# Column units as matmul pairs of 512 and 256 columns, their row scales later, and the first loads in quarters and halves

## The reference

```
x = x + 0.5 * swiglu(rms_norm(x), w_gate, w_up, w_down)        # "ffn1", inner width 2816
p = rms_norm(x) @ w_in                                          # "mix": RWKV-7 recurrence and pooled windows
x = x + concat(time_mix(p), pool_mix(p)) @ w_out
x = rms_norm(x + 0.5 * swiglu(rms_norm(x), ...))                # "ffn2", final norm of block 1
proj = rms_norm_2(x) @ w_in_2                                   # "mix2": rotary, sliding-window and differential attention
x = x + attention(proj) @ w_out_2
x = x + cross_attention(rms_norm_2(x), rms_norm_2(mem), w_cq, w_ckv, w_co)     # "mem", "cross"
x = x + square(relu(rms_norm_2(x) @ w_up)) @ w_down             # "mlp", inner width 4096
return rms_norm_2(x)
```

## Time and profile before

| | |
|---|---|
| median of three runs | 1076.35 us (1074.59 to 1076.88) |
| the profiled execution | 1075.12 us, of which the span from first to last instruction is 1073.2 us |
| PE busy | 1012.0 us, 94% of the span |
| DVE / ACT / POOL busy | 62% / 46% / 7% of the span |
| HBM read | 152.28 MB, 143 GB/s over the span |

### The profile page before, as it was taken

The page is one execution under the profiler, slowest core; times in us unless marked ns, Lnnn a source line. Parts: engine busy times, 40 slices in busy tenths (PEclk is TensorE's granted clock), DMA queues, the critical chain, the costliest instruction groups (busy, mean ns, idle before and its releaser), DMA issues.

```text
span 1073.2 us, 18930 instructions
## 1 busy us (share of the span) xinstructions
PE 1012.0 (94%) x7020; PEld 930.7 (87%) x7020; DVE 663.3 (62%) x1005; ACT 490.2 (46%) x806; POOL 70.5 (7%) x79
## 2 busy tenths in 40 slices
PE   7999999899799899999999999999999998999997
PEld 6899999798688886899999988998888887999996
DVE  4665555578894753765555577677646446555554
ACT  5544444566122121644444374533745545445542
POOL 3002000002240320000000000000300000000000
PEclk9999999999899999999999999999799998999999
DMA  6777656453310100576666746454034236565661
GB/s 200 213 238 219 185 178 190 122 158 100 97 41 2 39 2 1 167 209 192 178 191 179 235 118 190 140 169 161 20 98 138 79 99 196 180 191 178 194 190 64
DMA packets 204896, 154.01 MB, mean 144 GB/s; under 512 B 5947, under 2 KB 190624, under 8 KB 204848
## 3 DMA queue, kind: packets, MB, share of 16 engines
q1 hardware_dynamic: 203760, 151.35, 47.5%
q0 software_dynamic: 1088, 2.00, 0.7%
HBM read 152.28 MB, written 1.05 MB: 143 GB/s over the span
## 4 chain that ended last, share of the span: by engine, by line
PE 52%; ACT 3%; DVE 2%; DMA 1%; issue 1%; DVEq 0%; ACTq 0%
PE ps L458 52%; DMA raw<-in_w_ckv 1%; ACT XT L1062 1%; ACT arena L1047 1%; DVE wlo L1392 0%; ACT whi L1026 0%; PE ps L529 0%; ACT L1039 0%; DVE X L1411 0%; PE ps L792 0%; DVE X L1461 0%; DVE arena L1848 0%; DVE arena L1844 0%; ACT SMALL L1049 0%; DVE arena L1786 0%
## 5 line engine op out<-in xcount | busy, mean ns | idle before, releaser
L458 PE MATMUL ps<-XT,whi 128*128 128x256 f32 x2880 | 533.5, 287 | 7.7 <-DVE XT L1437 7.7
L458 PEld LDWEIGHTS ps<-XT,whi 128*128 128x128 f32 x2880 | 458.6, 193 | 17.6 <-issue 6.6
L1392 DVE TENSOR_TENSOR wlo<-raw,whi 128x1024 fp32r<-128x1024 f32 x280 | 343.7, 1231 | 151.5 <-ACT whi L1026 148.9
L458 PE MATMUL ps<-XT,wlo 128*128 128x256 f32 x1440 | 409.2, 284 | 0.0
L1026 ACT ACTIVATE whi<-raw 128x1024 fp32r<-128x1024 f32 x280 | 293.2, 1055 | 215.3 <-PE ps L458 127.7
L458 PEld LDWEIGHTS ps<-XT,wlo 128*128 128x128 f32 x1440 | 277.8, 193 | 0.0
L458 PE MATMUL ps<-whi,H 128*128 128x512 f32 x608 | 179.0, 395 | 5.9 <-DVE H L1952 4.0
L458 PE MATMUL ps<-arena 128*128 128x128 f32 (+7 forms) x1160 | 145.8, 298 | 14.0 <-DVE arena L1661 5.5
L458 PEld LDWEIGHTS ps<-arena 128*128 128x128 f32 (+3 forms) x1160 | 133.4, 192 | 28.1 <-DVE arena L1661 5.8
L458 PEld LDWEIGHTS ps<-whi,H 128*128 128x128 f32 x608 | 110.5, 191 | 25.5 <-DVE H L1952 4.2
L458 PE MATMUL ps<-wlo,H 128*128 128x512 f32 x304 | 96.0, 394 | 0.0
(11 more groups left out here) (232 smaller groups left out, 641.8 us busy)
## 6 DMA issues: line engine op xcount, KB each, us to landing
raw<-in_ffn_w_gate SPq DMA_DIRECT2D x44, 512.0 KB, 4.1
raw<-in_ffn_w_up SPq DMA_DIRECT2D x44, 512.0 KB, 3.8
raw<-in_ffn_w_down SPq DMA_DIRECT2D x44, 512.0 KB, 4.0
raw<-in_w_in SPq DMA_DIRECT2D x36, 512.0 KB, 3.9
raw<-in_w_up SPq DMA_DIRECT2D x32, 512.0 KB, 4.6
raw<-in_w_down SPq DMA_DIRECT2D x32, 512.0 KB, 3.5
raw<-in_w_out SPq DMA_DIRECT2D x16, 512.0 KB, 3.4
raw<-in_w_ckv SPq DMA_DIRECT2D x16, 512.0 KB, 5.1
```

The source lines that it names most:

```text
L458: return pe.matmul(o, st, mv, start=start, stop=stop, skip_group_check=True)
L1392: dve.tensor_tensor(wlo[:, n % RING, :], raw[:, n % RAW, :], whi[:, n % RING, :].bitcast(F32), sub).then_inc(lo_ready, 1)
```

## The change

- `a_unit`: per piece c one matmul of `whi` by all 512 columns of `XT[:, c, :]` into the whole bank, and one of `wlo` by the upper 256. The two halves of the bank are added afterwards: ACT copies the upper half of the bank out (`GL`, `UL`, `WLOW`, `CLOW`), DVE adds the lower half of the bank to it, and the row factor is multiplied in by a further instruction (ffn, mix, w_ckv keys), or folded into a later one (rotary tables, the copies of the values, the exponent's scale in cross).
- `row_scale` comes later: behind both units of chunk 0 in ffn, behind unit 2 in mix, behind unit 1 on mem; in cross it goes.
- mix: the multiplication by the row factor moves to POOL (`scale_rows`, 14 of 128 x 256), and the shift's two DVE instructions for unit k come one iteration later.
- x is loaded in four pieces and the first two units in two each, in the order x, gate, x, gate, up, up, and these are split as halves as they land; `wake` puts 8 and 10 small matmuls of constants ahead of the first real ones.
- `norm_hi` and `norm_lo` of mix, ffn2 and cross come ahead of the one split that stood before them; in mlp the sums go between chunks 1, 2 and 3, and `norm_scale` behind the last chunk.

```diff
@@ -382,10 +389,24 @@
...
-                sp.dma_start(X[:, tt, :], t["x"][0, tt * P:(tt + 1) * P, :]).then_inc(x_in[tt], 16)
-            for n in range(RAW):
-                load(n, 0, cols(("ffn1_w_gate", "ffn1_w_up")[n % 2], (n // 2) * P))
+            def load_half(n, h, src, landed):
+                dst = raw[:, n, 512 * h:512 * h + 512].rearrange("p (c n) -> p c n", c=KC // 2)
+                sp.dma_start(dst, src[:, 4 * h:4 * h + 4, :]).then_inc(landed, 16)
+            def load_x(h):
+                for tt in range(NT):
+                    sp.dma_start(X[:, tt, 512 * h:512 * h + 512],
+                                 t["x"][0, tt * P:(tt + 1) * P, 512 * h:512 * h + 512]).then_inc(x_in[2 * h + tt], 16)
+            load_x(0)
+            load_half(0, 0, cols("ffn1_w_gate", 0), raw_first[0])
+            load_x(1)
+            load_half(0, 1, cols("ffn1_w_gate", 0), raw_full[0])
+            load_half(1, 0, cols("ffn1_w_up", 0), raw_first[1])
+            load_half(1, 1, cols("ffn1_w_up", 0), raw_full[1])
+            load(2, 0, cols("ffn1_w_gate", P))
             def load_ffn(b, pre, first):
...
@@ -460,14 +481,19 @@
             def a_unit(n, dn, bank, after=None):
-                pe.wait_ge(lo_ready, n + 1 + dn)
+                halves = after == "ffn1" or (n == 1 and dn == 0)
+                if not halves:
+                    pe.wait_ge(lo_ready, n + 1 + dn)
                 s = n % RING
                 for c in range(KC):
+                    if halves and c == 0:
+                        pe.wait_ge(lo_first, n + 1)
+                    if halves and c == KC // 2:
+                        pe.wait_ge(lo_ready, n + 1)
                     if after and c % 2 == 0:
                         pe.wait_ge(xt_ready, 4 * NTP[after] + c // 2 + 1)
                     cs = slice(c * P, (c + 1) * P)
-                    mm(bank[:, 0:T], whi[:, s, cs], XT[:, c, 0:T], start=(c == 0), stop=False)
-                    mm(bank[:, 0:T], whi[:, s, cs], XT[:, c, T:2 * T], start=False, stop=False)
+                    mm(bank[:, :], whi[:, s, cs], XT[:, c, :], start=(c == 0), stop=False)
                     last = mm(bank[:, 0:T], wlo[:, s, cs], XT[:, c, 0:T], start=False, stop=(c == KC - 1))
                 last.then_inc(unit_used, 1)
...
@@ -538,8 +564,6 @@
                     if J + j >= 2:
                         pe.wait_ge(h_ready, J + j - 1 + dj)
                     a_unit(b + n, dn, PS[4 + j % 2], after)
-                    if after:
-                        row_scale(PS[0], RRB_N[after])
                     a_unit(b + n + 1, dn, PS[6 + j % 2])
                 def down(j, n, dn=0, dj=0, **k):
@@ -547,6 +571,7 @@
                     b_unit(b + n, dn, H[:, j % 2, :], **k)
                 gate_up(0, 0, after=("ffn1", "ffn2")[f])
+                row_scale(PS[0], RRB_N[("ffn1", "ffn2")[f]])
                 gate_up(1, 2)
                 pe.wait_ge(rrb_ready, RRB_N[("ffn1", "ffn2")[f]])
                 down(0, 4, start=True)
@@ -596,7 +621,7 @@
                     if i >= 4:
                         pe.wait_ge(w_sum, i - 3)
                     a_unit(B_WIN + i, 0, PS[W_BANKS[i % 4]], None if i else "mix")
-                    if i == 0:
+                    if i == 2:
                         row_scale(PS[0], RRB_N["mix"])
                     if i == 4:
                         pe.wait_ge(rrb_ready, RRB_N["mix"])
...
@@ -799,7 +824,7 @@
                     if i >= 4:
                         pe.wait_ge(c_sum, i - 3)
                     a_unit(B_CKV + i, 0, PS[Q_BANKS[i % 4]], None if i else "mem")
-                    if i == 0:
+                    if i == 1:
                         row_scale(PS[6], RRB_N["mem"])
                     if i == 5:
                         pe.wait_ge(rrb_ready, RRB_N["mem"])
...
+            def wake(n):
+                for k in range(n):
+                    mm(PS[k % 2][0:64, 0:P], ONES[:, 0:64], ONES)
+            pe.wait_ge(warm_set, 2)
+            wake(8)
             pe.wait_ge(const_in, 16)
             pe.wait_ge(first_in, 16)
             pe.transpose(PS[7][:, 0:KC], FIRST, ident[0:KC, 0:KC]).then_inc(vec_tp, 1)
+            wake(10)
             pe.wait_ge(vec_ready, 1)
             norm_t("ffn1")
             ffn(B_FFN1, 0)
...
@@ -1079,7 +1120,15 @@
                                 splits.n = n + 1
                     next_split(0)
+                    act.wait_ge(unit_used, b + n_gate + 1 + dn)
+                    if J + j >= 2:
+                        act.wait_ge(g_raw, J + j - 1 + dj)
+                    act.activation(GL[:, q, :], PS[4 + q][:, T:2 * T], ACT.Copy).then_inc(g_low, 1)
                     next_split(1)
+                    act.wait_ge(unit_used, b + n_up + 1 + dn)
+                    if J + j >= 2:
+                        act.wait_ge(u_sum, J + j - 1 + dj)
+                    act.activation(UL[:, q, :], PS[6 + q][:, T:2 * T], ACT.Copy).then_inc(u_low, 1)
                     act.wait_ge(g_sum, J + j + 1 + dj)
                     if J + j >= 2:
                         act.wait_ge(h_val, J + j - 1 + dj)
...
+            def low(i, n, bank, dst, sem_low, sem_sum, base=0):
+                split_to(n + LEAD + 1)
+                act.wait_ge(unit_used, n + 1)
+                if base + i >= 2:
+                    act.wait_ge(sem_sum, base + i - 1)
+                act.activation(dst[:, i % 2, :], bank[:, T:2 * T], ACT.Copy).then_inc(sem_low, 1)
             def deviation(wv):
...
@@ -1127,7 +1184,7 @@
             def mix():
                 row_scale(RRB_MIX, PS[0], RRB_N["mix"])
                 for i in range(N_WIN):
-                    split_to(B_WIN + i + LEAD + 1)
+                    low(i, B_WIN + i, PS[W_BANKS[i % 4]], WLOW, w_low, w_sum)
...
                 split_to(B_MLP + LEAD)
-                for j in range(3):
-                    chunk(j)
+                chunk(0)
+                chunk(1)
+                norm_sums(7, X, 6, [0])
+                chunk(2)
+                norm_sums(7, X, 6, [1])
                 with act.Fori(0, 9) as i:
...
@@ -1356,24 +1423,26 @@
             act.wait_ge(warm_set, 1)
             act.activation(SMALL[:, 346:347], WARM, ACT.Sqrt)
             act.wait_ge(const_in, 16)
-            split_to(1)
             act.wait_ge(vec_ready, 1)
             norm_hi("ffn1", "ffn1_norm")
+            split_half(1, 0)
+            split_half(1, 1)
+            splits.n = 2
+            split_to(3)
             norm_sums(0, X, 0)
             ffn(B_FFN1, 0)
             act.wait_ge(vec_ready, 2)
+            norm_hi("mix", "mix_norm")
             split_to(B_WIN + LEAD)
-            norm_hi("mix", "mix_norm")
             norm_sums(1, X, 1)
             mix()
...
-            norm_hi("ffn2", "ffn2_norm")
             norm_sums(2, X, 2)
...
             attention()
             cross()
             norm_hi("mlp", "g_mlp_2")
-            norm_sums(7, X, 6)
             mlp()
             norm_sums(8, X, 7)
...
@@ -1478,14 +1555,18 @@
                                 splits.n = n + 1
                     next_split(0)
-                    dve.wait_ge(unit_used, b + n_gate + 1 + dn)
+                    dve.wait_ge(g_low, J + j + 1 + dj)
                     if J + j >= 2:
                         dve.wait_ge(silu, J + j - 1 + dj)
-                    dve.tensor_tensor(GS[:, q, :], PS[4 + q][:, 0:T], RRB_FFN, mul).then_inc(g_sum, 1)
+                    dve.tensor_tensor(GS[:, q, :], PS[4 + q][:, 0:T], GL[:, q, :], add).then_inc(g_raw, 1)
+                    dve.wait_ge(g_raw, J + j + 1 + dj)
+                    dve.tensor_tensor(GS[:, q, :], GS[:, q, :], RRB_FFN, mul).then_inc(g_sum, 1)
                     next_split(1)
-                    dve.wait_ge(unit_used, b + n_up + 1 + dn)
+                    dve.wait_ge(u_low, J + j + 1 + dj)
+                    dve.tensor_tensor(US[:, q, :], PS[6 + q][:, 0:T], UL[:, q, :], add).then_inc(u_sum, 1)
+                    dve.wait_ge(u_sum, J + j + 1 + dj)
                     dve.wait_ge(silu, J + j + 1 + dj)
-                    dve.tensor_tensor(HS[:, q, :], PS[6 + q][:, 0:T], SG[:, q, :], mul).then_inc(h_val, 1)
+                    dve.tensor_tensor(HS[:, q, :], SG[:, q, :], US[:, q, :], mul).then_inc(h_val, 1)
                     dve.wait_ge(h_val, J + j + 1 + dj)
                     dve.wait_ge(h_hi, J + j + 1 + dj)
                     dve.tensor_tensor(H[:, q, T:2 * T], HS[:, q, :], H[:, q, 0:T].bitcast(F32),
...
+                def shift(k):
+                    dst = LBUF[:, k, :] if k < 2 else PV[:, k - 10, :] if k >= 10 else (PK, PR)[k % 2][:, (k - 2) // 2, :]
+                    mu = vec("mu_tail") if k == 1 else vec("mu_shift", WIN_COLS[k] // P)
+                    now, before = WRAW[:, k % 2, 1:T + 1], WRAW[:, k % 2, 0:T]
+                    dve.wait_ge(w_scaled, k + 1)
+                    dve.tensor_tensor(WDF[:, k % 2, :], before, now, sub).then_inc(own_dve, own.next())
+                    dve.wait_ge(own_dve, own.n)
```

(57 more changed lines are left out.)

139 lines of the change are left out of this document (86 added, 53 removed).

## The result

The changed kernel takes 1086.41 us (median of four runs, 1084.54 to 1087.26) against 1075.56 for the kernel before beside it (1074.59 to 1076.88). The ratio is 1.0098, with a 95% interval of 1.0078 to 1.0118. Forecast were 1073.2 us and a range of 1060 to 1083, so it is slower where faster was the likeliest, and outside the range. The profiled execution has a span of 1082.8 us against 1073.2. That of before is one of its faster ones: its granted clock is 0.979, where 24 of the 29 executions of before that were run beside the second group of experiments have 0.973 to 0.977.

A forecast was written before the change was run, and what follows sets the result against it. PE's pace was taken to bound mid-ffn1, with waits for DVE and ACT at joints and in mix. Terms -2.5 -3.6 +16 -1.2 -3.8 +1.5 +2.5 -2.6 -9.4 gave -3.1: 1073.2 us, range 1060 to 1083.

The forecast's parts named there:

- The pairs: Column units: a piece takes 0.349 us instead of 0.360, saving 0.09 per unit; ffn1 -3.6, ffn2 -3.8.
- Rival C: Column units: the pair doesn't pay and 113 path units lose their 0.09 us; 1083.4, chance 0.08.
- mem and w_in_2: Stages mem and w_in_2: no gain, PE's wait behind rope_args grows to about 6 us; +2.5, bounds 0 and +5.
- mlp: Stage mlp: wait before chunk 0 and half clock behind it go, 31 units get cheaper; -9.4 us, bounds -6 and -10.5.
- (a): Mix: row factors ready after unit 2 instead of unit 0, at 216.4 us instead of 214.26.
- (b): Mix: `w_mix` 2 takes three DVE iterations instead of two, 225.5 us instead of 220.2; PE waits 6.5.
- (d): Mix: `w_mix` 10 is raised one iteration later, ACT's activations follow the scans; K2 at 268.4 us instead of 257.16.
- (e): Mix: more POOL pauses and four multiplications, less what DVE waits for POOL today; +2.5 us.
- (c): Mix: POOL's products stretch DVE's iterations from 2.46 to 3.13 us, so the scans begin later; +3.7.
- Rival D: Start: the wake matmuls delay it by 2 us instead of the gain; 1077.7, chance 0.06.
- Rival A: Mix: the added work fits in DVE's and ACT's gaps, -5 us instead of +16; 1052, chance 0.13.
- Rival B: Mix and behind rope_args: granted clock falls longer than priced, 11.6 us instead of 3.0; 1082, chance 0.17.

The follow-up runs named there:

- second profile of after: The changed kernel run once more, unchanged, beside the kernel before: ratio 1.0075.
- the run with the kept parts: Changed kernel with column units of mix, mem and w_in_2 as before, mix's split ahead of the norm, mlp's sums between chunks 30 and 31: 0.9870 of before.

## Why the prediction was wrong

The sum was -3.1 and the trace has +9.6, 12.7 more; the second profile of after has +6.8. The table of joints says where, and the runs say why. No single term carries the miss: the pair is the largest one that is the same in every profile.

- **The pairs: the step that failed first, a term mis-sized (4.9 us).** "Per piece 0.229 + 0.120" took each interval from a stream of its own kind. Next to each other they are 0.236 + 0.117. 0.057 per unit instead of 0.09 is 1.3 less in ffn1 and 1.6 in ffn2. In mlp a unit and its row unit save 0.027 together, since there the row unit's matmuls, which were not changed, take 0.232 instead of 0.229: 2.0 less. The run with the pair alone has the same chunks without any added work. Rival C was half right, and had 0.08. The Trainium skill's fixed cost of about 2.5 ns per warm matmul (TensorE: Matmul & The Clock Gate, Wait — 56ns, not 53.3ns?) would give, by an estimate for 1440 matmuls fewer, under 4 us in all. The trace doesn't agree: 0.057 per unit is 7 ns for each matmul that goes, the prediction had 11, and the pair alone gave 11.6 us by the ratio.
- **The recurrence: a stretch left out of the sum (3.2).** No instruction in it was changed, so it stood at nothing. Around PE's wait of 4.70 at the end of mix and behind one of 2.73 in the recurrence, which before has too, the granted clock is at half from 291.0 to 297.9 and from 304.7 to 311.5, where before has 3.4 us at each place; further on it is three windows of 3.4 where before has two. In the second profile the stretch has lost 1.6. With mix as before, 2.8 of it is gone; with the waits filled too, the recurrence is 4.3 shorter (151.43 against 155.78, and 153.68 in before). That half clock is what it lost is shown by this; that mix's change brought it is not, since kernels with mix as before have between 152.98 and 155.78 here (the filled one left out) and those with the changed mix between 154.54 and 158.71. I had added 2.3 for the clock within mix and nothing behind it.
- **mem and w_in_2: mis-sized (2.5).** `rope_args` starts 3.0 later behind mem's first unit (27.51 against 24.49; 2.6 in the second profile); that was priced at "some 2". Seven multiplications of 0.43 would be 3.0, but the kernels that have all seven show 1.9 to 3.2, so that it is these and not the copies and sums of ACT is not shown. 1.7 more comes behind PE's wait of 7.20, at half clock (priced 0.7), and w_in_2 gives back 0.1 where 2.2 were counted. +5.0, at the upper bound. The run with the stage as before has both stretches back to 0.01.
- **mlp: a cost put at nothing (1.2).** The sums between chunks 1, 2 and 3 were taken as hidden because ACT is half idle. The chain to H, two instructions of ACT and three of DVE, takes 2.3 of the 5.6 us between the end of its column unit and its use, so by itself it has room. But ACT takes table load, square and root (905.74 to 908.51) and a split ahead of the copy, which starts at 909.46 for a unit that ended at 906.33, and DVE's addition stands behind a split that waited for ACT's (910.72). H is ready at 912.58, 6.25 behind its unit: chunks of 6.31 and 6.06. Put where ACT idles for 3.85 us it cost 0.2 at most. The wait of 3.98 and the half clock behind it went as forecast: the first row unit comes 3.8 sooner, and the step to the next falls from 8.55 to 5.67 (-2.9).
- **mix: right in size (+16.8 against +16), partly for the wrong reason.** (a) and (b) hold: LoRA's wait is 5.84 (6.5 forecast) and DVE's wait behind it 4.03. (d) holds: 6.7 between scans and K2 for 7.5, DVE waiting 6.28, and one moved call takes it back. (e) is 3.2 for 2.5. (c) is wrong. The scans are late, but POOL's pauses are covered: the iterations with LoRA products last 4.5 us, set by PE, in before (4.56) and, but for the first, in after. The rows could have told: seven iterations of 2.46 from 224.27 end at 241.5, and the scans of before start at 247.83. What made them late is half clock, 3.3 of 3.8. The row of the prediction that showed a difference of 2.17 for 0.42 was behind a product of 1024 columns; behind one of 256 it is 0.3 to 0.4. On this the Trainium skill (GPSIMD Engine Reference, Specifications) names the contention; trace and rule agree that it is there, and the run with the products on DVE takes the same time.
- **The norm ahead of the split: counted as a gain, it isn't one.** XT is 0.1 sooner, but ACT's sums stand 1.1 later behind the first unit, since the split that used to fill ACT's 2.1 us of waiting for the transposes is now behind them. In after this costs mix nothing: the diagonal is ready at 208.1, PE makes the row factors behind unit 2 at 209.8 without a wait, and ACT waits 2.98 for PE. With the row factors behind unit 0, as in the runs with mix as before, PE waits for the sums, and there it is 1.2 of the 2.6 that the first LoRA product was late; the run with the kept parts took them back. The other 1.4 went when the waits were filled.
- **The start: right and better (-3.7 for -2.5),** by the order, with the small matmuls worth 0.7 at most. Rival D fell.
- **ffn2's two ends: right** (-1.3 for -1.2, +1.7 for +1.5). **cross: -1.5 for -2.6;** PE's longest wait in the stage, behind the scores, grew from 1.61 to 2.54, which was not priced, and in the second profile of after the stage gains nothing (69.20).
- **Rival A** (mix costs nothing) fell with the first joint of mix. **Rival B** named the mechanism that the forecast under-priced. Filling five waits brought the ratio from 1.0098 and 1.0075 down to 1.0011.

The range failed with them: its upper end was the top of single rivals, though B and C exclude each other in nothing and each had a part.

Open is what makes up the 11.6 us of the pair alone beyond its chunks, why the interval between two matmuls depends on the neighbours as it does, and why mlp's row units grow. Nor do the runs show why the half clock falls in other places in two profiles of one kernel.

## What to carry to other kernels

Before a change trades matmuls for work elsewhere, list the in-order chains that have slack to take it. In ffn it was free. In mix a semaphore raised an iteration later, and between mlp's chunks the norm's sums, held up everything that stood behind them, and in mix and on mem half clock behind PE's waits came on top. Take the idle share of an engine for slack only where nothing that another engine waits for stands behind the added work. Price a wait of PE with what the clock does behind it, in the next stage too, and try to fill the wait: here six groups of constant matmuls brought the ratio from 0.9800 to 0.9752.

## What the runs showed that had not been expected

- The price of a matmul hangs on the order around it. With equal work a chunk took 8.39 (512, 256 in turn), 8.29 (two and two), 8.35 (four and four) and 8.31 us (eight and eight). The interval from a 256 to a 256 was 0.120 in before, and 0.1145, 0.118 and 0.119 in the groups.
- A row unit of mlp ran at 0.232 per matmul of 512 with the pairs beside it, and at 0.229 without, though nothing in it differs. In ffn it was 0.229 with and without them, and with the pairs in groups of two 0.228 in both.
- Small matmuls of constants that end 0.41 us before the real one kept the granted clock at 1.00 through a wait of 5.84 us; without them it was 0.50 for 10.2 us.
- Two profiles of the same kernel lay 2.8 us apart, with the clock at half in other places. A difference of 2 or 3 us in a stretch with such waits is not shown by one profile each.
